# Nine gate units per pair in place of ten, and the next pair's first two query projections placed in the last step of the pair before

## The reference, cut to what matters

```
h = _rmsnorm(x) * (1.0 + scale) + shift
qa, ka, va, za, qb, kb, vb, zb, ga, gb = split(h @ w_in)
oa = neighbourhood attention (8 heads, latent window and 512 cached context keys)
ob = sliding window attention with a sink (8 query heads, 2 key heads, rope, 512 cached keys)
ya = (oa * silu(za)) @ w_br_a
yb = (ob * silu(zb)) @ w_br_b
y  = x + gate * ((sigmoid(ga) * ya + sigmoid(gb) * yb) @ w_out)
return _rmsnorm(y) * final_norm_g
```

## Time and profile before

| | us |
|---|---|
| median of 3 runs | 1214.87 (1214.77 to 1215.3) |
| the profiled execution | 1214.08 |
| its span, first to last instruction | 1212.3 |
| TensorE busy | 1187.5 (98%) |
| VectorE busy | 819.3 (68%) |
| ScalarE busy | 601.3 (50%) |
| GpSimd busy | 92.4 (8%) |

### The profile page before, as it was taken

The page is one execution under the profiler, slowest core; times in us unless marked ns, Lnnn a source line. Parts: engine busy times, 40 slices in busy tenths (PEclk is TensorE's granted clock), DMA queues, the critical chain, the costliest instruction groups (busy, mean ns, idle before and its releaser), DMA issues.

```text
span 1212.3 us, 19668 instructions
## 1 busy us (share of the span) xinstructions
PE 1187.5 (98%) x7432; PEld 1076.8 (89%) x7432; DVE 819.3 (68%) x1596; ACT 601.3 (50%) x1205; POOL 92.4 (8%) x108
## 2 busy tenths in 40 slices
PE   7999999999999999999999999999999999999998
PEld 1799889989998998899899899989989988998996
DVE  4769458656765776587687597688779966454453
ACT  4632335535552654365465455555547675344342
POOL 0000000000000000000000000000000034533430
PEclk9999999999999999999999999999999999999999
DMA  9547702141123215022511121411113376642540
GB/s 362 178 175 226 231 30 72 45 135 61 40 79 96 64 40 162 22 72 69 139 63 46 49 63 41 134 39 58 38 40 124 113 233 211 204 152 95 201 146 35
DMA packets 71762, 132.81 MB, mean 110 GB/s; under 512 B 6774, under 2 KB 47734, under 8 KB 71676
## 3 DMA queue, kind: packets, MB, share of 16 engines
q1 hardware_dynamic: 57420, 109.70, 28.0%
q10 hardware_dynamic: 14256, 21.96, 5.0%
HBM read 96.24 MB, written 35.40 MB: 109 GB/s over the span
## 4 chain that ended last, share of the span: by engine, by line
PE 84%; DVE 9%; ACT 3%; issue 2%; DMA 1%; POOL 0%; ACTq 0%; SPq 0%; DVEq 0%
PE d_ps_pairs L84 23%; PE s_ps_pairs L84 12%; PE y_ps L1881 9%; PE o_ps_pairs L1070 9%; PE b_ps L84 8%; PE t_ps_pairs L1040 7%; PE v_ps L84 6%; PE s_ps_pairs L1004 4%; PE s_ps_pairs L1003 4%; DMA wada<-in_w_ada 1%; DVE pt L1401 1%; PE k_ps L352 1%; DVE mn L1407 1%; PE t_ps L344 1%; DVE q L1392 1%
## 5 line engine op out<-in xcount | busy, mean ns | idle before, releaser
L84 PE MATMUL d_ps_pairs<-h,wt 128*128 128x384 f32 (+2 forms) x1920 | 352.2, 338 | 0.9 <-ACT craw L1212 0.9
L84 PEld LDWEIGHTS d_ps_pairs<-h,wt 128*128 128x128 f32 x1920 | 316.7, 189 | 16.4 <-ACT craw L1212 1.9
L1401 DVE TENSOR_TENSOR pt<-t_ps_pairs,pt 128x512 fp32r<-128x512 f32 (+2 forms) x264 | 152.9, 619 | 64.7 <-ACT pt L1170 63.5
L84 PE MATMUL s_ps_pairs<-h,wt 128*128 128x512 f32 (+1 forms) x864 | 168.2, 354 | 0.0
L84 PEld LDWEIGHTS s_ps_pairs<-h,wt 128*128 128x128 f32 x864 | 141.6, 189 | 21.7
L1170 ACT ACTIVATE pt<-t_ps_pairs 128x512 fp32r<-128x512 f32 (+2 forms) x264 | 130.2, 544 | 16.8 <-PE t_ps_pairs L1040 11.5
L1194 ACT ACTIVATE pr<-s_ps_pairs,mx 128x896 f32<-128x896 f32 (+1 forms) x128 | 125.0, 982 | 26.9 <-DVE mx L1429 26.5
L1040 PE MATMUL t_ps_pairs<-ident_sb,pr 128*128 128x128 f32 x928 | 125.6, 274 | 1.9 <-DVE pt L1401 1.1
L1881 PE MATMUL y_ps<-wo,mg 128*128 128x512 f32 (+1 forms) x504 | 113.2, 385 | 0.0
L1040 PEld LDWEIGHTS t_ps_pairs<-ident_sb,pr 128*128 128x128 f32 x928 | 105.4, 140 | 8.8 <-DVE pt L1401 5.8
L1881 PEld LDWEIGHTS y_ps<-wo,mg 128*128 128x128 f32 x504 | 91.3, 188 | 20.6
(11 more groups left out here) (204 smaller groups left out, 1588.0 us busy)
## 6 DMA issues: line engine op xcount, KB each, us to landing
wraw<-in_w_gate SPq DMA_DIRECT2D x24, 512.0 KB, 3.8
gt<-gates_d SPq DMA_DIRECT2D x40, 256.0 KB, 4.5
gates_d<-craw ACTq DMA_DIRECT2D x48, 192.0 KB, 1.9
v_d<-vst SPq DMA_DIRECT2D x20, 320.0 KB, 4.6
wada<-in_w_ada SPq DMA_DIRECT2D x12, 512.0 KB, 9.8
oz<-gates_d SPq DMA_DIRECT2D x20, 256.0 KB, 4.6
oz<-o_d SPq DMA_DIRECT2D x20, 256.0 KB, 4.3
x_f<-in_x SPq DMA_DIRECT2D x10, 512.0 KB, 7.0
```

What stands on the lines that cost most here:

```text
L84: mm = eng.matmul(out, lhs(a, k), rhs(b, k), start=(k == 0 and i == 0), stop=(k == n_k - 1 and i == 2))
L1401: dve.tensor_tensor(pt[:, 1, c * 512:c * 512 + cols], t_ps[:, n % 2, 0:cols], pt[:, 0, c * 512:c * 512 + cols].bitcast(F32), ALU.subtract) ...
```

## The change

In three of the four pairs of each branch (not A3 and B3) the three gate blocks are cut into nine units of 428, 426 and 426 columns in place of ten of 512, 384 and 256; the number of columns is the same. Step 9 of these pairs has then no unit. In its place, and between the chunks, stand the first two projections of the next pair: `project` takes a range of the contraction's blocks, so that a projection can be cut in two. In branch a, the first projection (512 columns) is cut in halves, the second comes whole before `weighted(8, 1)`; in branch b the first (256 columns) is whole and the second (512 columns) is cut. ScalarE and VectorE take out the first projection (`projected(0, p + 1)`) before `tile_highs(9)`, and the second in the next pair's body as before, now without the first ahead of it. VectorE's `tile_lows(9)` moves ahead of `add_halves(8)`. The rest is counting of semaphores for units that are no longer ten to each pair.

```diff
-UNITS = [(0, 0, 512), (0, 512, 384), (0, 896, 384), (1, 0, 384), (1, 384, 384), (1, 768, 512),
-         (2, 0, 384), (2, 384, 384), (2, 768, 256), (2, 1024, 256)]
+UNITS9 = [(b, t0, n) for b in range(3) for t0, n in ((0, 428), (428, 426), (854, 426))]
+UNITS = [UNITS10 if p % PAIRS == PAIRS - 1 else UNITS9 for p in range(2 * PAIRS)]
...
+    TURN_K = KD // 2 if A else KD
...
-            for n in range(NG):
+            for n in range(0 if p == 0 else 2, NG):
                 if n == EARLY:
                     scores(0)
                 project(n)
+            ahead = p < PAIRS - 1
             for s in range(STEPS + 1):
+                turn = s == STEPS and ahead
                 if 0 < s < STEPS:
                     scores(s)
-                if 3 <= s < STEPS:
+                if turn:
+                    project(0, p + 1, 0, TURN_K)
+                if 3 <= s < STEPS or turn:
                     weighted(s - 2, 1)
-                if s == STEPS:
+                if s == STEPS and not ahead:
                     unit(s)
...
                 if s < STEPS:
                     unit(s)
+                elif not ahead:
+                    weighted(s - 2, 1)
+                elif TURN_K < KD:
+                    project(0, p + 1, TURN_K, KD)
                 else:
-                    weighted(s - 2, 1)
+                    project(1, p + 1, 0, KD // 2)
...
+            if ahead:
+                project(1, p + 1, 0 if TURN_K < KD else KD // 2, KD)
             weighted(STEPS - 1, 1)
...
             if last:
                 first_silu(act, f, 3)
+            if ahead:
+                projected(0, p + 1)
             if not last:
                 tile_highs(STEPS)
...
             if last:
                 first_gated(dve, f, 3)
+            if ahead:
+                projected(0, p + 1)
+            if not last:
+                tile_lows(STEPS)
             add_halves(STEPS - 1)
             if last:
                 tile_low_f(dve, f, 2)
-            if not last:
-                tile_lows(STEPS)
```

More of the change, by code:

```diff
@@ L68 @@
 GPP = 3
-UNITS = [(0, 0, 512), (0, 512, 384), (0, 896, 384), (1, 0, 384), (1, 384, 384), (1, 768, 512),
-         (2, 0, 384), (2, 384, 384), (2, 768, 256), (2, 1024, 256)]
-NU = len(UNITS)
-ENDS = [3, 6, 10]
+UNITS9 = [(b, t0, n) for b in range(3) for t0, n in ((0, 428), (428, 426), (854, 426))]
+UNITS10 = [(0, 0, 512), (0, 512, 384), (0, 896, 384), (1, 0, 384), (1, 384, 384), (1, 768, 512),
+           (2, 0, 384), (2, 384, 384), (2, 768, 256), (2, 1024, 256)]
+UNITS = [UNITS10 if p % PAIRS == PAIRS - 1 else UNITS9 for p in range(2 * PAIRS)]
+UNIT0 = [sum(len(u) for u in UNITS[:p]) for p in range(2 * PAIRS + 1)]
+ENDS = [[max(i for i, u in enumerate(units) if u[0] == b) + 1 for b in range(3)] for units in UNITS]
 STEPS = 9
@@ L77, with in_slot, split_mm @@
 CHUNKS_ALL = PAIRS * (NCHUNK["a"] + NCHUNK["b"])
-def split_mm(eng, out, lhs, rhs, n_k):
-    for k in range(n_k):
+def in_slot(slot, units):
+    return (units + 1 - slot) // 2
+def split_mm(eng, out, lhs, rhs, n_k, first=0, last=None):
+    for k in range(first, n_k if last is None else last):
         for i, (a, b) in enumerate(((0, 0), (0, 1), (1, 0))):
@@ L965, in body, with project @@
             pb = p + base
-            pe.wait_ge(exp_done, pb * 2 * STEPS)
-            def project(n):
+            def project(n, p=p, k0=0, k1=KD):
                 i, g, bank = PROJECTED[n]
                 t0, tn = GROUPS[g]
-                if n % 3 == 0:
+                if n == 0 and k0 == 0:
+                    pe.wait_ge(exp_done, (p + base) * 2 * STEPS)
+                if n % 3 == 0 and k0 == 0:
                     pe.wait_ge(w_lo, ready(p, i))
@@ L1127, in split_values, with projected @@
                                ACT.Copy).then_inc(cvh, 1)
-            def projected(n):
+            def projected(n, p=p):
                 _, g, bank = PROJECTED[n]
@@ L1218, in tile_high @@
                 if A:
[L1219 to L1223 removed]
+                    sem, value = [(proj_done, p * NG + 3), (proj_done, p * NG + 6), (d_done, UNIT0[pb] + ENDS[pb][0]),
+                                  (d_done, UNIT0[pb] + ENDS[pb][1]), (d_done, UNIT0[pb] + ENDS[pb][2])][n]
+                else:
+                    sem, value = [(d_done, UNIT0[pb]), (proj_done, p * NG + 3), (d_done, UNIT0[pb] + ENDS[pb][0]),
+                                  (d_done, UNIT0[pb] + ENDS[pb][1 if last else 2])][n]
                 act.wait_ge(sem, value)
@@ L1252, in body @@
                     exps(0)
-                projected(n)
+                if n > 0 or p == 0:
+                    projected(n)
             if not A and fresh(p):
@@ L1258, in body @@
                 act.dma_start(io["new_ak"][p], kout[:, :]).then_inc(ko_out, 16)
+            ahead = p < PAIRS - 1
             for s in range(STEPS + 1):
-                if s == STEPS:
+                ends = s == STEPS and not ahead
+                if ends:
                     gate(s)
@@ L1273, in body @@
                     high(s - 1, range(2, chunks[s - 1]))
-                gate_out(s)
+                if s < len(UNITS[pb]):
+                    gate_out(s)
                 if s < STEPS:
@@ L1525, in body @@
                 split_values()
+            ahead = p < PAIRS - 1
             for s in range(STEPS + 1):
+                ends = s == STEPS and not ahead
                 if 0 < s < STEPS:
                     minima(s)
-                if 2 <= s < STEPS:
+                if s >= 2 and not ends:
                     add_halves(s - 2)
@@ L1710, in _ @@
         sp.wait_ge(m_done, ALL * 2 * STEPS)
-        sp.wait_ge(g_out[0], (ALL - 1) * HALF * 16)
-        sp.wait_ge(g_out[1], (ALL - 1) * HALF * 16)
+        for slot in range(2):
+            sp.wait_ge(g_out[slot], in_slot(slot, UNIT0[ALL - 1]) * 16)
         load_gt(0, 0)
         load_gt(0, 1)
-        sp.wait_ge(g_out[0], ALL * HALF * 16)
-        sp.wait_ge(g_out[1], ALL * HALF * 16)
+        for slot in range(2):
+            sp.wait_ge(g_out[slot], in_slot(slot, UNIT0[ALL]) * 16)
         load_w(5)
```

39 lines of the change are left out of this document (19 added, 20 removed).

## The result

The change takes 1222.15 us (median of 4 runs, 1221.15 to 1225.41) against 1214.82 for the kernel before (4 runs): ratio 1.0068 [1.0056, 1.0079]. It is 0.7% slower, above the range that the prediction gave. The profiled execution took 1225.41 us.

What follows compares the result with a forecast made beforehand. The prediction took TensorE, busy 1187.5 of 1212.3 us, to bound the kernel. Its terms, -2.0 - 7.1 + 4.3 + 4.9 + 0.3 = +0.4 on 1214.87, gave 1215.3 us, with a range of 1213 to 1217.5.

Steps and rivals of the forecast that it cites:

- The waits at pairs' ends (-7.1): TensorE's waits in each pair's last step go entirely: 3 x 1.1 us in branch a, 3 x 1.27 in branch b.
- The cuts: Projections cut by transposes change TensorE's kind of work more often: 0.05 us per transition, +0.3 us for six.
- The wait in branch a (+4.3): TensorE waits 1.4 us before the fifth projection for VectorE's last `projected(1)` operation, at three transitions.
- The wait in branch b (+4.9): ScalarE's later copy of projection 1 delays VectorE's prompt reduction: 1.15 us at B0-B1 and B2-B3, 2.6 at B1-B2.
- Ten units made nine save 0.33 us in each of six pairs: A unit fewer saves the width-independent part of its 24 matmuls on TensorE: -2.0 us in all.
- the nine units save nothing: Rival: no width-independent saving at 428 columns, or odd starts read slower; 1217.3 to 1219 us, chance 0.07.
- the clock falls at the new waits: Rival: TensorE's granted clock falls at each of six transitions, 7.2 us more, 1222.5 us; chance 0.10.

Runs made afterwards that it cites:

- experiment 1: The change's new orders with the ten old units in every pair, against the kernel before: 1218.82 us, ratio 1.0043.
- experiment 2: The changed kernel with the next pair's cached keys and values split ahead of `low_half(8)` in branch a alone: 1220.27 us, 1.0048 to the kernel before.
- Experiment 3: The changed kernel with unit 0 of B0 and B2 staged in slot 0, the half of `craw` holding the keys: 1220.33 us, 1.0046 to the kernel before.
- Experiments 5: The changed kernel with other unit widths: 448 + 416 + 416 took 1222.26 us; 512 + 384 + 384, the one read at B1, 1219.25 us.
- experiment 6: The best kernel (orders and staging mended, units 512 + 384 + 384) with the first block of B0 to B2 cut 384 + 512 + 384: 1210.8 us.

## Why the prediction was wrong

Its sum was +0.4. The measured intervals of the table add up to 11.6 us, the steps to 0.4. Step by step:

- **The waits at pairs' ends (-7.1): right.** They are gone; up to the fifth projection's wait the rows above show no idle time, and with the ten old units (experiment 1) B0-B1 fell by 1.09. The cuts cost a little more than 0.05: from 243.05 to 258.01 are 14.96 us for 14.75 of work at the paces of before.
- **The wait in branch a (+4.3): right**, 1.42 against 1.4, at the named instruction and with the named releaser; experiment 2 took it away.
- **The wait in branch b (+4.9): right.** B3's idle time grew by 1.22 (1.15 predicted). In the change B1's is 0.25 + 1.15 + 0.72 for the narrower first unit = 2.12, measured 2.13. With ten units the same orders gave +1.20 and +2.54.
- **"Ten units made nine save 0.33 us in each of six pairs" (-2.0): failed.** The step took the fixed part from units in rows 4 and laid the line through 428. The chain's rows show 4.19 for 384 columns; by distance of starts a unit ahead of transposes takes 4.27, and one of 512 takes 5.57. Units of 426 and 428 take 4.72 in the change, but for those behind the falls and one of 4.80, also as first unit, where the prediction's line gives 4.60. Nine are 42.48 us; the ten took 42.39, so a pair gained nothing and lost about 0.1. With 512 + 384 + 384 nine take about 0.2 less than ten. I had allowed 0.1 a unit, 5 us, as a bound and held it unlikely. A unit did come out 0.12 over the line, but the old units ahead of transposes lie 0.08 to 0.13 over it too, so half of the 5 is left. This term of the sum is the step that failed: 0.12 of the 0.42 a pair is the saving itself (0.2 with widths of 512 and 384, not 0.33), 0.3 the widths between. That is the rival "the nine units save nothing", to which I gave 0.07. Cost against the sum: 6 x 0.42 = 2.5.
- **Overlooked, a term put at nothing: the staging slot.** I read the diff's counting as bookkeeping ("the rest is counting of semaphores"). An odd number of units turns the slot's parity, and in B0 and B2 the copy waits 1.52 for another engine: 3.0. Experiment 3 shows it in the trace.
- **The clock: a rival that came true.** I gave 0.10 to "the clock falls at the new waits", and let it decide the sign from two falls on. It fell three times in the profiled execution: 1.59 + 1.60 + 1.81 = 5.0. The rival's total, 1222.5, is near the measured 1222.15 by chance: it had six falls of 1.2 and neither the slot nor the widths. The 1.2 was too low, since the stretch of the earlier trace rows ends within the fall: the kernel before has 0.50 from 37.70 to 41.00, too. What else I had not seen is that the staging and the narrow first unit would make the waits 3.75 and 5.47 long. Experiments 5 (at B1) and 6 (at B2) moved the idle time of a second unit down and up, and the fall went and came with it, in one profiled execution each. That the clock fell there is shown by the rows with 0.50; what length of wait suffices is not. The Trainium skill (TensorE: Matmul & The Clock Gate, What's actually happening) has the array slow when it has been idle; the rows agree (0.50 in B0's second unit, behind 3.75 us of idle time).
- **The late load in B0**, 0.8 in this execution. In experiments 2, 3 and 5 the second unit of B0 is at most 0.3 later than the other terms make it. Why the load was late stays open.

Together 2.5 + 3.0 + 5.0 + 0.8 = 11.3 above the steps, where the table has 11.2. Stretch by stretch it closes less well: with the falls, the slot and the late load taken off, branch a is 0.45 to 0.54 above its steps, branch b 0.40, 0.17, 0.26 and 0.11, where the widths should give 0.42 in each of the three pairs with nine units. The other runs of the change, at clocks of 0.995 to 0.997, were 2.9 to 4.3 us faster than the profiled one, which speaks for fewer falls in them. Then the median's excess of 6.9 over the forecast is the widths and the staging (5.5) and about one fall. Those runs left no trace, but the table without the clock agrees: 5.7 above the kernel before, where 0.4 + 2.5 + 3.0 are 5.9.

## What to carry to other kernels

When a change alters how many pieces go through a double buffer, follow the parity to the next use of that buffer: a semaphore count that looks like bookkeeping picks which engine is waited for. A cost per instruction read from a line through three widths holds for the place it was read in; take it from the rows that have the same neighbour. And on TensorE price a wait twice, once by its length and once by what the next product takes behind it; where pieces of unlike width are to be placed, a wide one ahead of the wait is the better order (experiment 6).

## What the runs showed of the hardware

Over the twelve profiled kernels there are 36 second units in B0 to B2. In the 18 with an idle time of 0.5 to 2.0 us none was slow. Of the 18 with 2.1 to 5.5 us, 16 were slow, by 1.2 to 2.7 us; two, with 3.10 and 3.23 in B0, ran at full pace. In the change's pairs B0 to B2 the granted clock was 0.97 to 0.98 where it was 1.00 otherwise; within the units it was 0.50, the 1.2 GHz level. The loss is not in proportion to the wait: 1.6 behind 2.13 and 1.8 behind 5.47. It depends on where the fall begins. In B0 the unit had run for over 1.2 us at 1.00 before the clock fell, with TensorE busy; in B2 2.9 us of the time at 0.50 lay in the wait, where they cost nothing. So look at what follows a wait and not only at the wait. Two executions of one kernel can differ by whole falls: 4.3 us lie between the fastest and the slowest run of the change.
